# Low parts of weights: a GpSimd subtraction, or a negated copy and an adding transfer

## The reference

```python
proj = jnp.einsum("bsd,dn->bsn", h, w_in)
q, k, v, f_logit, g_b, g_c, hc, gate_conv, gate_attn = jnp.split(proj, _SPLITS, axis=-1)
ya = g_b * causal_depthwise_conv(g_c * hc, conv_w)
yb = forgetting_attention(q, k, v, logf)
merged = sigmoid(gate_conv) * (ya @ w_branch[0]) + sigmoid(gate_attn) * (yb @ w_branch[1])
x = x + rmsnorm(merged @ w_out, norm_mix_post)
g, u = jnp.split(rmsnorm(x, norm_ffn_pre) @ w_gate_up, 2, axis=-1)
x = x + rmsnorm((silu(g) * u) @ w_down, norm_ffn_post)
```

## Time and profile before

| | us |
|---|---|
| median of 3 runs | 1313.55 |
| lowest and highest | 1313.33, 1314.04 |
| the profiled execution | 1313.93 |
| its span, first to last instruction | 1312.1 |
| TensorE busy | 1297.1 |
| VectorE busy | 794.8 |
| ScalarE busy | 613.1 |
| GpSimd busy | 298.3 |

### The profile page before, as it was taken

One profiled execution on the slowest core, in us unless ns is written; L12 is line 12 of the kernel. 1 busy time (PEld: TensorE's weight loads), 2 busy tenths in 40 slices (PEclk: granted clock), 3 DMA queues, 4 the chain that ended last, 5 costly groups with the idle time before them and its releaser, 6 DMA issues.

```text
span 1312.1 us, 18344 instructions
## 1 busy us (share of the span) xinstructions
PE 1297.1 (99%) x7158; PEld 1084.9 (83%) x7158; DVE 794.8 (61%) x1577; ACT 613.1 (47%) x1300; POOL 298.3 (23%) x203
## 2 busy tenths in 40 slices
PE   8999999999999999999999999999999999999999
PEld 6778888888889999998887887888788878887787
DVE  4425664333479887887333647576767667677743
ACT  4335654333435444445223445555556555656531
POOL 2022310000055556540001412131222223131010
PEclk9999999999999999999999999999999999999999
DMA  6322232332533234243236322222222222223511
GB/s 229 105 57 73 57 96 65 97 96 96 204 118 111 85 127 121 73 130 112 73 104 209 113 65 67 94 73 72 80 80 95 77 73 73 74 72 133 196 33 65
DMA packets 110297, 130.35 MB, mean 99 GB/s; under 512 B 7553, under 2 KB 87425, under 8 KB 110210
## 3 DMA queue, kind: packets, MB, share of 16 engines
q1 hardware_dynamic: 104450, 112.39, 26.6%
q10 hardware_dynamic: 5760, 16.78, 3.6%
HBM read 119.72 MB, written 9.44 MB: 98 GB/s over the span
## 4 chain that ended last, share of the span: by engine, by line
PE 86%; DVE 6%; issue 4%; ACT 2%; POOL 1%; DMA 0%; ACTq 0%; DVEq 0%; POOLq 0%
PE ps L845 14%; PE ps L847 14%; PE ps L846 13%; PE ps L850 7%; PE ps L852 6%; PE ps L851 6%; PE ps L1069 5%; PE ps L1072 5%; PE ps L1071 5%; PE ps L1127 2%; DVE wlo L1506 1%; PE ps L1137 1%; PE ps L1109 1%; PE ps L1161 1%; PE ps L973 1%
## 5 line engine op out<-in xcount | busy, mean ns | idle before, releaser
L1506 DVE TENSOR_TENSOR wlo<-raw,whi 128x512 fp32r<-128x512 f32 (+1 forms) x294 | 232.8, 818 | 186.0 <-ACT whi L1191 185.3
L1191 ACT ACTIVATE whi<-raw 128x512 fp32r<-128x512 f32 (+2 forms) x338 | 208.7, 650 | 118.6 <-PE ps L847 87.7
L845 PE MATMUL ps<-whi,hth 128*128 128x512 f32 x592 | 244.2, 413 | 0.1
L847 PE MATMUL ps<-wlo,hth 128*128 128x512 f32 x592 | 231.4, 391 | 0.0
L846 PE MATMUL ps<-whi,htl 128*128 128x512 f32 x592 | 231.1, 390 | 0.0
L1926 POOL TENSOR_TENSOR wlo<-raw,whi 128x384 fp32r<-128x384 f32 (+1 forms) x44 | 49.4, 1140 | 428.2 <-ACT whi L1191 428.2
L845 PEld LDWEIGHTS ps<-whi,hth 128*128 128x128 f32 x592 | 111.3, 188 | 32.6 <-issue 9.2
L847 PEld LDWEIGHTS ps<-wlo,hth 128*128 128x128 f32 x592 | 111.1, 188 | 24.7
L846 PEld LDWEIGHTS ps<-whi,htl 128*128 128x128 f32 x592 | 111.6, 189 | 18.6
L1456 ACT ACTIVATE px<-px,nm 128x128 f32<-128x128 f32 (+3 forms) x128 | 70.7, 554 | 90.4 <-DVE nm L1839 87.1
L850 PE MATMUL ps<-hth,whi 128*128 128x512 f32 (+1 forms) x288 | 112.0, 389 | 0.0
(11 more groups left out here) (347 smaller groups left out, 2860.4 us busy)
## 6 DMA issues: line engine op xcount, KB each, us to landing
raw<-in_l_w_in SPq DMA_DIRECT2D x64, 512.0 KB, 4.7
raw<-in_w_gate_up SPq DMA_DIRECT2D x44, 512.0 KB, 4.8
raw<-in_w_in SPq DMA_DIRECT2D x13, 1024.0 KB, 5.3
raw<-in_w_down SPq DMA_DIRECT2D x10, 1024.0 KB, 5.1
raw<-in_l_w_out SPq DMA_DIRECT2D x8, 1024.0 KB, 5.2
raw<-in_w_in SPq DMA_DIRECT2D x26, 256.0 KB, 3.7
raw<-in_w_branch SPq DMA_DIRECT2D x8, 512.0 KB, 4.2
raw<-in_w_out SPq DMA_DIRECT2D x4, 1024.0 KB, 5.1
```

The source lines that it names most:

```text
L845: e.matmul(o, ah, wh[:, cs], start=a, stop=False)
L847: m = e.matmul(o, ah, wl[:, cs], start=False, stop=z)
L1191: return e.activation(out, in_, ACT.Copy, **how)
L1506: return e.tensor_tensor(out, src, hi_part.bitcast(F32), ALU.subtract)
```

## The change

For the halves with `h.pool`, the low part is no longer made by a subtraction. ScalarE, right behind the rounded copy of a chunk, copies the raw chunk once more, with a scale of -1, into the low tile: the negated rounded value. When two chunks are there, GpSimd issues one transfer from the raw tile to the low tile with `accum_op=ALU.add`, which adds the raw values to what stands there. One transfer serves two chunks: 128x768 (384 KB) in the convolution's halves, 128x1024 (512 KB) in the others. There are 22 of them. Two semaphores per pair of tiles, one for each half of a low tile, tell that a transfer has landed; TensorE waits for them in `three`, and SP waits for both before it loads a raw tile anew.

```diff
+                if W.h[n].pool and c == 0:
+                    accs[W.h[n].slot] += 1
+                    self.acc[n] = accs[W.h[n].slot]
...
-        mm, hi, lod, lop = sem("mm"), sem("hi"), sem("lo_dve"), sem("lo_pool")
+        mm, hi, lod, neg_hi = sem("mm"), sem("hi"), sem("lo_dve"), sem("neg_hi")
+        lo_acc = [[sem(f"lo_acc{i}{half}") for half in range(2)] for i in range(2)]
...
-                    pe.wait_ge(lop if h.pool else lod, order.lo[n, kt // h.step])
+                    if h.pool:
+                        pe.wait_ge(lo_acc[h.slot][kt // h.step // 2], 16 * order.acc[n])
+                    else:
+                        pe.wait_ge(lod, order.lo[n, kt // h.step])
...
                     copy(wide(n)[0][:, cs], raw[n % 3][:, cs]).then_inc(hi, 1)
+                    if h.pool:
+                        copy(wide(n)[1][:, cs], raw[n % 3][:, cs], scale=-1.0).then_inc(neg_hi, 1)
...
-                    whole_hi, whole_lo = wide(n)
-                    pool.wait_ge(hi, order.hi[n, c])
-                    e.tensor_tensor(whole_lo[:, cs], raw[n % 3][:, cs], whole_hi[:, cs].bitcast(F32),
-                                    ALU.subtract).then_inc(lop, 1)
+                    if c % 2:
+                        cs = slice(chunk(n, c - 1).start, cs.stop)
+                        pool.wait_ge(neg_hi, order.lo[n, c])
+                        e.dma_start(wide(n)[1][:, cs].bitcast(F32), raw[n % 3][:, cs], accum_op=ALU.add).then_inc(
+                            lo_acc[H[n].slot][c // 2], 16)
...
-                        sp.wait_ge(lop if q.pool else lod, order.lo[n - 3, (q.nk - 1) // q.step])
+                        if q.pool:
+                            for half in range(2):
+                                sp.wait_ge(lo_acc[q.slot][half], 16 * order.acc[n - 3])
+                        else:
+                            sp.wait_ge(lod, order.lo[n - 3, (q.nk - 1) // q.step])
```

More of the change, by code:

```diff
@@ L188, in __init__ @@
                 h.behind = self.mm[h.behind if isinstance(h.behind, tuple) else W.h[h.behind].last]
-        self.hi, self.lo = {}, {}
-        count = [0, 0]
+        self.hi, self.lo, self.acc = {}, {}, {}
+        count, accs = [0, 0], [0, 0]
         for s in self.steps:
```

## The result

The changed kernel takes 1323.59 us (median of 4 runs, 1322.77 to 1324.02); the kernel before, measured beside it, 1313.47. The ratio on record is 1.0072 with a 95% interval of 1.0060 to 1.0083 (the two medians alone give 1.0077): slower by 10 us, where 11.9 were forecast (1325.4).

What follows compares the result with a forecast made beforehand. TensorE's own work was taken as the bound, busy 1297.1 of 1312.1 us. Stalls 9.4, clock 1.7 and boundaries 1.0 made 12.1, of which 11.9 was kept: 1313.55 + 11.9 = 1325.4 us, range 1317 to 1341.

Steps and rivals of the forecast that it cites:

- What bounds it: Whole kernel: TensorE's own work bounds it, 1297.1 of 1312.1 us; removing the 44 subtractions gains 0.
- L: Time from the end of a pair's second negated copy until TensorE may go on; taken as 4.7 us.
- Half 4: Fifth of the convolution stage's eight weight halves (0 to 7): slack -0.5 us, TensorE stalls 5.2 us.
- half 6: Seventh of the convolution stage's eight weight halves: slack 2.8 us, TensorE stalls 1.9 us.
- half 2: Third of the convolution stage's eight weight halves: slack 3.5 us, TensorE stalls 1.2 us.
- Half 7: Last of the convolution stage's eight weight halves: slack 3.8 us, TensorE stalls 0.9 us.
- A stall is not paid back: Convolution stage: ScalarE's work behind a stall waits for TensorE's steps and moves along; stalls sum to 9.4 us.
- The clock: Behind the stall of half 4, the only one longer than 2.1 us, TensorE's granted clock drops: +1.7 us.
- The boundaries: A negated copy of 0.52 us enters the chain before TensorE at each of two boundaries: +1.0 us.
- Crowded transfers: Rival, transfers crowded or starved: L about 9.2 us, stalls 41.4, total 1368 us; chance 0.11.

Runs made afterwards that it cites:

- the last experiment: The changed kernel with halves 4 and 6 made by subtraction, all other transfers kept: 1317.30 us, ratio 1.0021.
- the copies alone: The kernel before with the 44 negated copies added on ScalarE, GpSimd waiting for them and still subtracting: 1317.76 us, ratio 1.0029.
- the slack version: The changed kernel with transfers only in halves 0, 1, 3 and 5, the other seven halves by subtraction: 1314.15 us, ratio 1.0000.
- the early order with subtractions: The kernel before with the splits of these halves put earlier in the order, subtractions kept: 1314.95 us, ratio 1.0003.

## Why the prediction was right

- **What bounds it**: right. TensorE's 100.00 us of the stage left nothing to gain, and VectorE's freed time gave nothing.
- **L**: 4.7 taken, 4.3 to 4.5 measured where TensorE waited. By its parts: the transfer from issue to landing 4.0 (4.4 taken, the issue of 1.0 included; it was 0.87 and is part of the 4.0), hand-overs 0.3 to 0.4 (0.3). A plain one takes 2.6 from issue, 2.96 from the copy's end to TensorE. The Trainium skill ("DMA: Bandwidth & Descriptors", Anatomy of one DMA) gives, as an estimate from its 2.0 us and 436 GB/s, 2.9 for these bytes. The plain transfer agrees within 0.3; the adding one took 1.1 more than that from its issue.
- **Half 4**: 5.2 forecast, 4.6 measured. Its ScalarE run was delayed by four copies as worked out. Of the 0.6 too much, 0.2 is L's. Another 0.2 is in the slack: the forecast counted it to the load of the weights, 0.23 ahead of the matmul, but behind a wait the load and the matmul start together, both at 146.70, so this lead isn't lost. The same holds for half 6 (1.9 against 1.4) and half 2 (1.2 against 0.6).
- **Half 7**: 0.9 forecast, 0 measured. The step that failed is "A stall is not paid back": half 6's stall paid for half 7, whose loss of 0.8 appears in the last experiment. That this term and the lead above went wrong in the same direction as L is why the stalls came out 2.6 too high.
- **The clock**: the drop behind half 4's stall came as forecast and cost 1.7. Between the two profiled executions it is mostly cancelled by the drop near 424 that before's had the earlier trace rows and the changed one's had not. In the medians it isn't. Traces without a drop after the first 15 us have a mean clock of 1.0, those with one drop of 3.4 us 0.998 or 0.999, and the one with two such drops 0.997. In the later measurements 35 of 49 runs of the kernel before have 1.0 (medians 1313.45 to 1313.47) and 14 have 0.999 (1314.95 to 1315.2); all four of the changed kernel lie below 1.0, at 0.997 to 0.999. The 10.1 us of the medians less 7.8 that the trace shows as stalls (6.6), attention (0.3) and boundaries (0.9) leave 2.3, an estimate of what the clock adds to the median, where 1.7 were forecast; it takes the starts as alike.
- **The boundaries**: 1.0 forecast, 0.9 measured.
- **Crowded transfers**: they did occur, 7.4 us for one pair of the stage and 8.3 and 8.2 at the boundaries, but only where nothing waited for them. The forecast had given the case 0.11 as if it held for all.
- **Left out**: 0.3 us at an attention product near 224 us. Its cause is not shown. No negated copy stands near it; it appears in all six traces in which half 4 has negated copies and in none of the four others. And 1.3 us of late start in the profiled execution, which is not the change's.

Between the two profiled executions the errors partly cancel: 2.6 too much in the stalls (9.2 against 6.6), 0.1 in the boundaries and 1.4 in the clock, against 0.3 and 1.3 left out. What remains is 11.9 forecast and 9.4 in the spans, 10.1 in the medians. The mechanism and the place of the largest stall were right. That the total came within 2 us is in part luck, since terms left out made up for terms too high.

## What to carry to other kernels

Moving an operation off an engine that nothing waits for gained nothing here, and what replaces it must be judged by its latency at the one consumer that is just in time, not by its work. List for each consumer the slack between the producer's end and the wait, and compare the new latency with each: here four pairs of the stage's sixteen (both of half 2, the second of halves 4 and 6) made all its stalls, and eight others were free when only they were transfers. A pair that is in time only because TensorE has just stalled is not safe: it comes out late when the stall before it is mended. A transfer that covers two chunks makes the first wait for the second. And a median over few runs can differ by the clock alone by 1.5 to 2 us, so differences of 1 us are to be read in the traces or between runs of equal clock.

## What was not expected of the hardware

- An adding transfer of 384 KB within the core's memory landed 4.0 us after its issue by GpSimd, a plain one 2.6 (medians of 16). Adding ones of 192 KB took 3.0 when no other of GpSimd's overlapped, of 512 KB 4.5 to 4.6 in the shortest three cases. Beside a crowd of other transfers they took 7.4 (384 KB) and 8.3 (512 KB), and plain ones 6.8 and 7.1.
- The clock drop behind a wait of 2.1 us of TensorE (L1069) comes in some executions and not in others: seven of the eleven traces have it, those of the changed kernel, of the copies alone, of the slack version and of the early order with subtractions don't. Runs of one kernel at a mean clock of 1.0 are 1.5 to 2 us faster than those below. The wait of 4.4 or 4.5 us at half 4 had a drop in both traces that have it, one of 2.4, in the kernel with one transfer per chunk, had it too; one of 3.0 in the profiled execution of the kernel with plain transfers did not, nor did one of 0.6 in the kernel with the copies alone.
